# The second block's mixer: the sums of the softmaxes as a 65th column of the value products

## The chip, the cores and the metric

The kernel runs on one core of a Trainium2 chip. The metric is the device time of one execution in microseconds, as the median of three runs. TensorE (PE in the profile) multiplies and transposes, ScalarE (ACT) copies and applies functions, VectorE (DVE) does elementwise work and reductions, GpSimd (POOL) helps with powers, and the sync engine (SP) issues the loads. Each engine works through its own list in order; semaphores tie the lists together.

## The reference, cut to what matters

Two blocks of two layers each follow one another over 256 tokens of width 1024. The change lies in the mixer of the second block, which runs in both of its layers and holds three kinds of attention:

```python
# latent attention, 6 heads, causal
o_a = mla_causal_attention(q_a, k_a, kvh[..., MLA_NOPE:])
# differential attention, 6 heads: softmax(q1 k1) - lam * softmax(q2 k2), with distance slopes
p = probs(q1, k1) - lam * probs(q2, k2)
return jnp.einsum('bhqk,bhkd->bhqd', p.astype(v.dtype), v)
# block attention, 4 heads of 64; at 256 tokens it is one causal block
p = jax.nn.softmax(jnp.concatenate([s_sel, s_own], axis=-1), axis=-1).astype(v.dtype)
```

Every head has values 64 wide, and every output row is the product of the exponentials with the values, divided by the sum of the row's exponentials. A softmax row thus needs that sum, and nothing else of the sum is used. The mixer is followed by a cross attention over a memory and by an MLP. All matrix products of weights are made of three products of high and low parts; those of the attention are plain fp32.

## The kernel before, in words

**Tiling.** The 256 tokens are two tiles of 128 (t = 0, 1). Activations lie with tokens on the partitions (`X`, `H`, `proj`), and transposed where they are multiplied with weights (`HTh`, `HTl`). Weights come by DMA into a ring, ScalarE copies each piece to its high part `Wh` (L1724), VectorE subtracts to get the low part `Wl` (L2227), and TensorE makes three products a tile of rows (L922 to L924).

**The mixer.** The input projection has five blocks of columns (`IN2_BLOCKS`). ScalarE copies each out of PSUM into `proj` with the row's scale: `take_block` for blocks 0 to 3 (L1770 in the profile, since a helper records it) and `take_last` for block 4 (L2117), one instruction a tile. Between them lie the products of the latents (L983), whose results `take_heads` copies (L2130), the sums of squares of the latents on VectorE (L3021) and their scaling (L3026). The values of the differential heads lie in `proj` at column 1184, those of the block heads at column 2080, and those of the latent heads in `VV`, all 64 wide and one behind the other.

**A unit** of attention is one tile of 128 queries and up to four heads (`unit`, L362). It has kl keys: 128 for t = 0 and 256 for t = 1. The mixer has twelve units a layer: six differential ones (0 to 5), two of the block attention (6, 7), four of the latent attention (8 to 11, the last two with two heads). They hold 44 heads a layer. A unit passes through these steps, and the engines work on different units at a time:
- TensorE multiplies queries and keys (`scores`, L1075);
- VectorE adds bias or mask into `SM`, takes the maximum and writes its negative to `nb` (`mask`, L2378 to L2388);
- ScalarE takes the exponentials in `SM`, head by head, and has each summed into `sums` by the instruction's accumulator (`exps`, L1817);
- TensorE transposes the exponentials by blocks of 128 keys (`probs`, L1087), and other tiles that are due (L1097), and ScalarE copies them out of PSUM into `PT` (`copies`, L1829) or elsewhere (L1836);
- TensorE multiplies the transposed exponentials, as weights, with the values, 64 columns a head and block of keys (`values`, L1130), into one bank of PSUM;
- VectorE takes the reciprocals of `sums` and scales the product with them (`end`, L2411 to L2423).

**What sets the order.** It is written out by hand. TensorE's loop (`finish`) puts, for step i, the scores of unit i, then what `amid` names for the step, then the transposes of unit i-1, then the values of unit i-2. `amid` holds the fifth block of the input projection in quarters at steps 1 to 4 (products of 384 columns) and three products each at steps 5 to 11 whose result nobody reads (`unread`, L1653; fillers below). ScalarE's loop has the copies of unit i-1, `take_last` at steps 2 and 4, the exponentials of unit i, and weight splits after steps 0 and 4. VectorE's loop has the mask of unit i, weight splits at steps 0, 2 and 5, and the outputs of unit i-2.

Of the kernel before, what the change touches and what calls it, by code (L numbers as in the profile page):

```python
# [32 lines left out]
P = 128  # L33
# [62 lines left out]
C1W = 28 + CC * TAPS  # L96
C2 = dict(attn=0, cross=8, mem=16, mlp=24, qn=32, kvn=34)
C2W = 35
B1W = 4 * HD
B2W = HD + 4 * DIFF_D  # L100

# [9 lines left out]
def build(nc, a, out):  # L111
    ctx = ExitStack()
    with ctx:
        def sb(name, shape, dt=F32):
            return ctx.enter_context(nc.sbuf_tensor(name, shape, dt))
# [13 lines left out]
        HTh = sb("HTh", [P, KC, S], F32R)  # L129
        HTl = sb("HTl", [P, KC, S], F32R)  # L130
        proj_at = nc.sbuf_base
        proj = sb("proj", [P, T, IN2])
        scr_at = nc.sbuf_base
        scr = sb("scr", [P, 6656])

# [66 lines left out]
        CQT = QT[:, 12:15, :]  # L202
        KN = H[:, :, 0:MLA_H * NOPE].rearrange("p t (h d) -> p t h d", d=NOPE)
        QN = proj[:, :, 0:MLA_H * NOPE].rearrange("p t (h d) -> p t h d", d=NOPE)
        VV = scr[:, 22 * S:25 * S].rearrange("p (t h d) -> p t h d", t=T, h=MLA_H)
        QR = scr[:, 18 * S:21 * S].rearrange("p (t h d) -> p t h d", t=T, h=2 * MLA_H)
        KR4 = H[:, :, 768:896].rearrange("p t (n d) -> p t n d", n=4)
        MEM = scr[:, 0:T * D].rearrange("p (t d) -> p t d", t=T)
# [151 lines left out]
        def unit(t, kl, scores, bias, scale, values, dv, end, dst, kbs=None, needs=0, one=True):  # L360

            n = len(scores)  # L362
            apart = 2 if n == 2 and dv < P else 1
            return dict(t=t, kl=kl, one=one, scores=scores, bias=bias, scale=scale, values=values, dv=dv, end=end, dst=dst,
                        kbs=kbs or [P] * (kl // P), needs=needs, slots=slice(0, n * apart, apart))

        def o_bank(un, u):
# [65 lines left out]
        def diff_units(layer):  # L433
            out_ = []
            for ha, hb in ((0, 2), (1, 3), (4, 5)):
                for t in range(T):
                    kl = (t + 1) * P
                    sc, val, slopes = [], [], []
                    scale = DIFF_D ** -0.5
                    for k in range(2):  # L440
                        for h in (ha, hb):
                            r, slot = (64 * (h % 2) + k * DIFF_D, h // 2) if h < 4 else (k * DIFF_D, h - 2)
                            sc.append([(QT[r:r + DIFF_D, slot, tok(t)], QT[r:r + DIFF_D, 4 + slot, 0:kl])])
                            val.append([proj[:, kb, DV0 + h * 64:DV0 + h * 64 + 64] for kb in range(t + 1)])
                            slopes.append(-SLOPES[h] / scale)
                    dst = heads_of(H[:, t, 384:768], DIFF_H)[:, ha:hb + 1:hb - ha, :]
                    out_.append(unit(t, kl, sc, ("slopes", dist[:, t, 0:kl], slopes), scale, val, 64, ("diff", layer), dst))
            return out_

        def moba_units():  # L450
            out_ = []
            for t in range(T):
                kl = (t + 1) * P
                sc, val = [], []
                order = [2 * b + a for a in range(2) for b in range(2)]
                for h in order:
                    r = 64 * (h % 2)
                    sc.append([(QT[r:r + 64, 8 + h // 2, tok(t)], QT[r:r + 64, 10 + h // 2, 0:kl])])
                    val.append([proj[:, kb, MV0 + h * 64:MV0 + h * 64 + 64] for kb in range(t + 1)])
                scale = 64 ** -0.5  # L460
                bias = ("slopes", dist[:, t, 0:kl], [-SLOPES[DIFF_H + h] / scale for h in order])
                dst = H[:, t, 768:1024].rearrange("p (b a d) -> p a b d", a=2, b=2)
                out_.append(unit(t, kl, sc, bias, scale, val, 64, ("plain",), dst, needs=4))
            return out_
# [56 lines left out]
        for c0, slot in ((DQ0, 0), (DK0, 4)):  # L521
            t_diff.append(chunks_batch([plain_chunk(proj, c0), plain_chunk(proj, c0 + P)], slot))
            t_diff.append(chunks_batch([plain_chunk(proj, c0 + 256, 64), plain_chunk(proj, c0 + 320, 64)], slot + 2, 64))
        t_moba = [chunks_batch([plain_chunk(proj, c0 + P * b) for b in range(2)], slot)
                  for c0, slot in ((MQ0, 8), (MK0, 10))]
        qn, kn = ([plain_chunk(src, P * b) for b in range(3)] for src in (proj, H))
        qr = [plain_chunk(QR.rearrange("p t h d -> p t (h d)"), P * b) for b in range(3)]
        kr = [plain_chunk(H, 768)]
# [373 lines left out]
        def _(pe):  # L902
# [152 lines left out]
            def attention(units, extras={}, tail=None, amid={}):  # L1055
# [62 lines left out]
                def values(i):  # L1118
                    u, un = u0 + i, units[i]
                    if un["end"][0] == "nsa":  # L1120
                        return values_turned(i)
                    pe.wait_ge(pt_out, first[i] + len(un["kbs"]))
                    if un["one"] and u >= 1:
                        pe.wait_ge(o_out, u)
                    elif u >= 2:
                        pe.wait_ge(o_out, u - 1)
                    dv = un["dv"]
                    for m, vs in enumerate(un["values"]):
                        for kb, v in enumerate(vs):
                            mm = pe.matmul(PS[:, o_bank(un, u), m * dv:(m + 1) * dv],  # L1130
                                           PT[0:un["kbs"][kb], u % 2, kb, m, :], v,
                                           start=(kb == 0), stop=(kb == len(vs) - 1))
                    mm.then_inc(o_full, 1)
# [576 lines left out]
        def _(act):  # L1710
# [93 lines left out]
            def attention(units, extras={}, meanwhile={}, ahead_of={}):  # L1804
# [5 lines left out]
                def exps(i):  # L1810
                    u, un = u0 + i, units[i]
                    act.wait_ge(sm_ready, u + 1)
                    if u >= 4:
                        act.wait_ge(o_out, u - 3)
                    for m in range(len(un["scores"])):
                        row = SM[:, u % 2, m, 0:un["kl"]]
                        ins = act.activation(row, row, ACT.Exp, bias=nb[:, u % 2, m:m + 1], scale=un["scale"],  # L1817
                                             accum_out=sums[:, u % 4, m:m + 1])
                    ins.then_inc(p_ready, 1)
# [281 lines left out]
            for layer in range(LAYERS):  # L2101
                if layer == 0:
                    act.activation(st[:, 0:8], ident[:, 0:8], ACT.Exp)
                    ahead()
                    norm(col2(layer, "attn", 8), BY_HALF)

                def take_block(k):
                    c0, n = IN2_BLOCKS[k]
                    for t in range(T):
                        take(proj[:, t, c0:c0 + n], scale=row_rs[:, 0, t:t + 1])  # L2110

                def take_last(t):

                    c0, n = IN2_BLOCKS[4]
                    c.lin += 1
                    act.wait_ge(lin_full, c.lin)
                    act.activation(proj[:, t, c0:c0 + n], PS[:, 6, 0:n], ACT.Copy,  # L2117
                                   scale=row_rs[:, 0, t:t + 1]).then_inc(lin_out, 1)

                def take_heads(parts, width):  # L2120

# [16 lines left out]
                for k in range(4):  # L2138
                    c.piece += 2
                    ahead()  # L2140
                    if k == 0:
                        row_scale()
                    take_block(k)
                    if k == 1:
                        turn(t_latent(layer))
                    elif k == 2:
                        take_heads((QN, QR), NOPE + MROPE)
                        turn(t_diff)
                    elif k == 3:
                        take_heads((KN, VV), NOPE + MLA_V)  # L2150
                attention(diff_units(layer) + moba_units() + mla_units(), mix_extras,
                          {0: another, 4: another}, {2: lambda: take_last(0), 4: lambda: take_last(1)})
                turn_mix(t_mixed)
# [50 lines left out]
        def _(dve):  # L2204
# [155 lines left out]
            def attention(units, extras={}, between=None, early={}):  # L2360
# [45 lines left out]
                def end(i):  # L2406
                    u, un = u0 + i, units[i]
                    n, dv, t, dst, kind = len(un["scores"]), un["dv"], un["t"], un["dst"], un["end"]
                    dve.wait_ge(o_full, u + 1)
                    cf = coef[:, u % 2, 0:n]  # L2410
                    seq(dve.reciprocal(cf, sums[:, u % 4, 0:n]))  # L2411
                    o = heads_of(PS[:, o_bank(un, u), 0:n * dv], n)
                    tmp = otmp[:].rearrange("p (m d) -> p m d", m=4)
                    if kind[0] == "plain":
                        by = bc4(cf, dv)
                        if len(dst.shape) == 4:
                            o = o.rearrange("p (a b) d -> p a b d", a=2)
                            by = cf.rearrange("p (a b) -> p a b", a=2).unsqueeze(3).to_broadcast(list(dst.shape))
                        dve.tensor_tensor(dst, o, by, ALU.mult).then_inc(o_out, 1)
                    elif kind[0] == "diff":  # L2420
                        seq(dve.tensor_tensor(cf, cf, lam4[:, kind[1], :], ALU.mult))
                        seq(dve.tensor_tensor(tmp, o, bc4(cf, dv), ALU.mult))
                        dve.tensor_tensor(dst, tmp[:, 0:2, :], tmp[:, 2:4, :], ALU.add).then_inc(o_out, 1)  # L2423
# [575 lines left out]
            for layer in range(LAYERS):  # L2999
# [14 lines left out]
                c.piece += 2  # L3014
                ahead()
                dve.wait_ge(lin_out, base + 2)
                parts = [(t, c0, n, 2 * t + i) for t in range(T) for i, (c0, n) in enumerate(((0, QRANK), (CKV0, KVR)))]
                junk = SM[:].rearrange("p a b c -> p (a b c)")
                for t, c0, n, o in parts:
# [129 lines left out]
```

## Time and profile before

| | |
|---|---|
| time, median of 3 runs | 2428.24 us (2427.86 to 2430.18) |
| span of the profiled execution | 2425.3 us |
| TensorE busy | 2375.5 us, 98% |
| VectorE busy | 1730.3 us, 71% |
| ScalarE busy | 1447.4 us, 60% |
| mixer's attention, layer 0 / layer 1 | about 1600 to 1662 us / 2035 to 2097 us |

The time of a run is a little longer than the span of the profile, which runs from the first to the last recorded instruction. In a timeline, the first number is the start and the second the duration; where several like instructions are merged ("x4"), the duration is from the first's start to the last's end. What stands in brackets is idle time of the engine before it and what ended it. A matmul's end is modelled and lies after the start of the next one, since they are pipelined: how fast TensorE goes is read from the distance of starts. An fp32 product leaves two records, a transpose one.

### The profile page before, as it was taken

What the parts mean: (1) busy time and instruction counts of PE and PEld (TensorE: products, weight loads), DVE (VectorE), ACT (ScalarE), POOL (GpSimd) and SP (SyncE); (2) the same over time, 40 slices, a digit from 0 to 9 for tenths busy, and PEclk for the clock granted to TensorE, in tenths of its full rate; (3) what the DMA queues carried; (4) which work ended last, traced back from release to release, by engine and by line L of the source; (5) the groups of instructions that cost most, each with busy time, mean ns of one, the idle gap of its engine ahead of it and who ended that gap; (6) DMA issues with size and microseconds to landing.
All of it is one profiled execution on the core that took longest, in us unless ns stands there. A gap on an engine that the chain in (4) does not pass through costs nothing.

```text
span 2425.3 us, 32059 instructions
## 1 busy us (share of the span) xinstructions
PE 2375.5 (98%) x12122; PEld 1950.6 (80%) x12122; DVE 1730.3 (71%) x2103; ACT 1447.4 (60%) x1761; POOL 85.7 (4%) x87
## 2 busy tenths in 40 slices
PE   9899999899999999999999999999999999999998
PEld 8578888667888888888888888888878888887887
DVE  7665446758988888898888898767455565755555
ACT  6544444547777777777777777665544446554443
POOL 1100000201000000000000000001000000000000
PEclk9999999989999999999999999999999999999999
DMA  7435555327999999999999999715535542453551
GB/s 261 159 127 188 191 190 159 121 93 256 360 352 366 347 372 350 368 349 369 347 370 344 373 348 371 242 54 184 182 122 190 182 149 87 158 190 105 191 191 44
DMA packets 249705, 569.99 MB, mean 235 GB/s; under 512 B 9664, under 2 KB 20352, under 8 KB 249600
## 3 DMA queue, kind: packets, MB, share of 16 engines
q1 hardware_dynamic: 249456, 568.30, 66.6%
q8 instruction: 70, 1.15, 0.2%
q14 instruction: 35, 0.29, 0.0%
q10 hardware_dynamic: 144, 0.26, 0.0%
HBM read 562.82 MB, written 1.05 MB: 232 GB/s over the span
## 4 chain that ended last, share of the span: by engine, by line
PE 93%; DVE 4%; ACT 2%; issue 1%; POOLq 0%; POOL 0%; ACTq 0%; DVEq 0%
PE PS L922 26%; PE PS L924 26%; PE PS L923 26%; PE PS L1075 2%; PE PS L1087 1%; PE PS L1545 1%; PE PS L1130 1%; PE PS L1374 1%; PE PS L994 1%; PE PS L1194 1%; PE PS L1113 1%; ACT SM L1817 1%; PE PS L1019 1%; PE PS L1335 1%; PE PS L983 1%
## 5 line engine op out<-in xcount | busy, mean ns | idle before, releaser
L2656 DVE TENSOR_TENSOR Wl<-ring,Wh 128x2048 fp32r<-128x2048 f32 x334 | 761.8, 2298 | 101.0 <-ACT Wh L1963 101.0
L1963 ACT ACTIVATE Wh<-ring 128x2048 fp32r<-128x2048 f32 x334 | 639.9, 1919 | 127.7 <-PE PS L924 127.7
L2227 DVE TENSOR_TENSOR Wl<-ring,Wh 128x2048 fp32r<-128x2048 f32 (+2 forms) x192 | 431.3, 2251 | 283.4 <-ACT Wh L1724 282.9
L1724 ACT ACTIVATE Wh<-ring 128x2048 fp32r<-128x2048 f32 (+2 forms) x192 | 361.5, 1890 | 237.5 <-PE PS L924 236.7
L922 PE MATMUL PS<-Wh,HTh 128*128 128x512 f32 (+3 forms) x1184 | 465.6, 393 | 4.2 <-DVE Wl L2227 2.4
L924 PE MATMUL PS<-Wh,HTl 128*128 128x512 f32 (+3 forms) x1184 | 457.5, 386 | 0.0
L923 PE MATMUL PS<-Wl,HTh 128*128 128x512 f32 (+3 forms) x1184 | 456.6, 386 | 0.0
L922 PE MATMUL PS<-Wh,xgh 128*128 128x512 f32 x896 | 354.6, 396 | 1.8 <-DVE Wl L2656 1.2
L924 PE MATMUL PS<-Wh,xgl 128*128 128x512 f32 x896 | 349.8, 390 | 0.0
L923 PE MATMUL PS<-Wl,xgh 128*128 128x512 f32 x896 | 349.2, 390 | 0.0
L922 PEld LDWEIGHTS PS<-Wh,HTh 128*128 128x128 f32 x1184 | 223.6, 189 | 50.2 <-issue 4.2
L924 PEld LDWEIGHTS PS<-Wh,HTl 128*128 128x128 f32 x1184 | 223.2, 188 | 43.7
L923 PEld LDWEIGHTS PS<-Wl,HTh 128*128 128x128 f32 x1184 | 223.8, 189 | 40.8
L922 PEld LDWEIGHTS PS<-Wh,xgh 128*128 128x128 f32 x896 | 168.4, 188 | 37.4 <-DVE Wl L2656 2.0
L924 PEld LDWEIGHTS PS<-Wh,xgl 128*128 128x128 f32 x896 | 168.3, 188 | 35.8
L923 PEld LDWEIGHTS PS<-Wl,xgh 128*128 128x128 f32 x896 | 168.6, 188 | 33.4
L922 PE MATMUL PS<-Wh,hmh 128*128 128x512 f32 x448 | 176.0, 393 | 0.7 <-DVE hml L2670 0.7
L924 PE MATMUL PS<-Wh,hml 128*128 128x512 f32 x448 | 174.6, 390 | 0.0
L923 PE MATMUL PS<-Wl,hmh 128*128 128x512 f32 x448 | 174.5, 389 | 0.0
L922 PE MATMUL PS<-Wh,hTh 128*128 128x512 f32 x368 | 143.8, 391 | 0.0
L924 PE MATMUL PS<-Wh,hTl 128*128 128x512 f32 x368 | 143.4, 390 | 0.0
L923 PE MATMUL PS<-Wl,hTh 128*128 128x512 f32 x368 | 143.3, 389 | 0.0
(346 smaller groups left out, 2469.3 us busy)
## 6 DMA issues: line engine op xcount, KB each, us to landing
ring<-in_moe_w_gate SPq DMA_DIRECT2D x112, 1024.0 KB, 7.1
ring<-in_moe_w_up SPq DMA_DIRECT2D x112, 1024.0 KB, 7.6
ring<-in_moe_w_down SPq DMA_DIRECT2D x112, 1024.0 KB, 7.1
ring<-in_mlp_w SPq DMA_DIRECT2D x64, 1024.0 KB, 5.3
ring<-in_w_in SPq DMA_DIRECT2D x27, 1024.0 KB, 5.2
ring<-in_w_out SPq DMA_DIRECT2D x16, 1024.0 KB, 6.9
ring<-in_cross_wkv SPq DMA_DIRECT2D x16, 1024.0 KB, 12.3
ring<-in_ffn_w_gate SPq DMA_DIRECT2D x14, 1024.0 KB, 5.1
```

The costliest lines, as they stand in the source:

```text
L922: pe.matmul(out_, hi, high, start=start, stop=False)
L923: pe.matmul(out_, hi, low, start=False, stop=False)
L924: return pe.matmul(out_, lo, high, start=False, stop=stop)
L983: mm = pe.matmul(PS[:, bank, 0:n], lhs(kc, t), w[:, kc, c0:c0 + n], start=(kc == 0), stop=(kc == k - 1))
L994: mm = pe.transpose(PS[0:width, c.turn % 4, off:off + rows], s, ident[0:rows, 0:rows])
L1019: mm = pe.transpose(PS[:, 2 * t + half, i * P:i * P + P], src[:, t, kc * P:kc * P + P], ident[:])
L1075: mm = pe.matmul(PS[:, 2 * (u % 2) + at[m] // 2, (at[m] % 2) * S:(at[m] % 2) * S + un["kl"]], q, key, start=(k == 0), stop=(k == len(un["s ...
L1087: mm = pe.transpose(PS[0:size, 4 + x % 2, m * P:m * P + P], SM[:, u % 2, m, kb * P:kb * P + size], ident[:])
L1724: act.activation(Wh[:, i % SPLITS, 0:n], ring[:, r % RING, 0:n], ACT.Copy).then_inc(w_hi, 1)
L1963: act.activation(Wh[:, (base + i) % SPLITS, :], ring[:, (raw + i) % RING, :], ACT.Copy).then_inc(e_hi, 1)
L2227: dve.tensor_tensor(Wl[:, i % SPLITS, 0:n], ring[:, r % RING, 0:n], Wh[:, i % SPLITS, 0:n].bitcast(F32), ALU.subtract).then_inc(w_lo, 1)
L2656: dve.tensor_tensor(Wl[:, (base + i) % SPLITS, :], ring[:, (raw + i) % RING, :], Wh[:, (base + i) % SPLITS, :].bitcast(F32), ALU.subtract) ...
```

## The change

A column of ones is put behind the 64 values of each head, so that the value product gives 65 columns and the last one is the sum of the row's exponentials. What follows from that:
- `proj` is laid out anew: heads of differential and block values are 65 apart (`DVS`, `MVS`), `VV` too. `proj` grows by 12 columns a tile, which moves everything behind it in SBUF by 96 bytes.
- The copies of blocks 2, 3 and 4 of the projection become two instructions a tile, one for the heads of values and one for the rest (six more a layer).
- VectorE writes the ones with six memsets a layer, ahead of the latents' sums of squares.
- The exponentials of the mixer's units have no accumulator and no wait on `o_out`. Those of the first block and of the cross attention are as before.
- The value products have 65 columns a head, and the reciprocal reads column 64 of each head in PSUM.

```diff
@@ unit
+            wide = VW if one and end[0] != "nsa" else dv
+            return dict(t=t, kl=kl, one=one, wide=wide, summed=wide > dv, scores=scores, ...
@@ values, on TensorE
-                    dv = un["dv"]
+                    wide = un["wide"]
                     for m, vs in enumerate(un["values"]):
                         for kb, v in enumerate(vs):
-                            mm = pe.matmul(PS[:, o_bank(un, u), m * dv:(m + 1) * dv],
+                            mm = pe.matmul(PS[:, o_bank(un, u), m * wide:(m + 1) * wide],
@@ exps, on ScalarE
-                    if u >= 4:
+                    if u >= 4 and not un["summed"]:
                         act.wait_ge(o_out, u - 3)
                     for m in range(len(un["scores"])):
                         row = SM[:, u % 2, m, 0:un["kl"]]
+                        if un["summed"]:
+                            ins = act.activation(row, row, ACT.Exp, bias=nb[:, u % 2, m:m + 1], scale=un["scale"])
+                            continue
@@ ScalarE's copies of the projection
+                def spread_heads(dst, src, rs_t):
+
+                    return act.activation(dst, src.rearrange("p (h d) -> p h d", d=64), ACT.Copy, scale=rs_t)
...
+                        if k == 2:
+                            spread_heads(DVS[:, t, 0:4, 0:64], src[:, 256:512], rs_t)
+                            act.activation(proj[:, t, c0:c0 + 256], src[:, 0:256], ACT.Copy, scale=rs_t).then_inc(lin_out, 1)
+                        else:
+                            spread_heads(DVS[:, t, 4:6, 0:64], src[:, 0:128], rs_t)
+                            act.activation(proj[:, t, MQ_AT:MQ_AT + 384], src[:, 128:512], ACT.Copy,
+                                           scale=rs_t).then_inc(lin_out, 1)
...
-                    act.activation(proj[:, t, c0:c0 + n], PS[:, 6, 0:n], ACT.Copy,
-                                   scale=row_rs[:, 0, t:t + 1]).then_inc(lin_out, 1)
+                    act.activation(proj[:, t, MK_AT + 128:MK_AT + 256], PS[:, 6, 0:128], ACT.Copy, scale=rs_t)
+                    spread_heads(MVS[:, t, :, 0:64], PS[:, 6, 128:384], rs_t).then_inc(lin_out, 1)
@@ end, on VectorE
-                    seq(dve.reciprocal(cf, sums[:, u % 4, 0:n]))
-                    o = heads_of(PS[:, o_bank(un, u), 0:n * dv], n)
+                    o = heads_of(PS[:, o_bank(un, u), 0:n * un["wide"]], n)
+                    seq(dve.reciprocal(cf, o[:, :, dv] if un["summed"] else sums[:, u % 4, 0:n]))
+                    o = o[:, :, 0:dv]
@@ VectorE, ahead of the latents' sums of squares
                 dve.wait_ge(lin_out, base + 2)
+                for values_ in (DVS, MVS, VV):
+                    for t in range(T):
+                        dve.memset(values_[:, t, :, VW - 1:VW], 1.0)
```

ScalarE's list from the exponentials of unit 0 to those of unit 2, before (the row of an exponential stands for the ACTIVATE and its read of the accumulator; `Wh` is a weight split):

```order
L1817 ACTIVATE SM,sums<-SM,nb 128x128 x4
L1724 ACTIVATE Wh<-ring 128x2048
L1817 ACTIVATE SM,sums<-SM,nb 128x256 x4
L1829 ACTIVATE PT<-PS 128x512
L1836 ACTIVATE scr<-PS 128x512
L1829 ACTIVATE PT<-PS 128x512 x2
L2117 ACTIVATE proj<-PS,row_rs 128x384
L1817 ACTIVATE SM,sums<-SM,nb 128x128 x4
```

The same stretch of the changed kernel:

```order
L1827 ACTIVATE SM<-SM,nb 128x128 x4
L1733 ACTIVATE Wh<-ring 128x2048
L1827 ACTIVATE SM<-SM,nb 128x256 x4
L1841 ACTIVATE PT<-PS 128x512
L1848 ACTIVATE scr<-PS 128x512
L1841 ACTIVATE PT<-PS 128x512 x2
L2147 ACTIVATE proj<-PS,row_rs 128x128
L2121 ACTIVATE proj<-PS,row_rs 128x4x64
L1827 ACTIVATE SM<-SM,nb 128x128 x4
```

The exponentials write no sums, and the copy of the late block (L2117) has become two instructions; the order of the rest is as it was.

VectorE's list at the latents of layer 0, before (`ISA` are the sums of squares and the reads of their accumulators):

```order
L2267 TENSOR_SCALAR mean_sq<-mean_sq 128x2
L2227 TENSOR_TENSOR Wl<-ring,Wh 128x2048 x2
L3021 ISA SM,st<-proj 128x256
L3021 ISA st 128x1
L3021 ISA SM,st<-proj 128x128
```

And in the changed kernel:

```order
L2297 TENSOR_SCALAR mean_sq<-mean_sq 128x2
L2257 TENSOR_TENSOR Wl<-ring,Wh 128x2048 x2
L3050 MEMSET proj 128x6 x2
L3050 MEMSET proj 128x4 x2
L3050 MEMSET scr 128x6 x2
L3055 ISA SM,st<-proj 128x256
L3055 ISA st 128x1
L3055 ISA SM,st<-proj 128x128
```

Six memsets have been put between the two weight splits and the sums of squares.

## Rows read from the trace of the kernel before

**Rows 1.** Page, chain that ended last: share of the span by engine.
```profile
PE 93%; DVE 4%; ACT 2%; issue 1%; POOLq 0%; POOL 0%; ACTq 0%; DVEq 0%
```

**Rows 2.** Waits of TensorE in 1600 to 1662 us: total, times, longest.
```profile
PE PS L1130 <- DVE H L2419: 0.7, 1, 0.7
PE PS L1097 <- ACT PT L1829: 0.5, 2, 0.3
```

**Rows 3.** Groups of ScalarE by form: busy us, mean ns | idle before.
```profile
L1817 ACT ACTIVATION_READ_ACCUMULATOR SM<-SM,nb 128x1 f32 x200 | 38.0, 190 | 0.0
...
L1770 ACT ACTIVATE proj<-PS,row_rs 128x512 f32<-128x512 f32 x32 | 21.9, 690 | 31.9 <-PE PS L924 31.9
...
L2055 ACT ACTIVATE proj<-PS,row_rs 128x256 f32<-128x256 f32 x4 | 1.9, 470 | 3.8 <-PE PS L924 3.8
```

**Rows 4.** Timeline of ScalarE in the mixer, layer 0.
```profile
1585.23 0.33 ACT L2130 ACTIVATE proj<-PS 128x192 f32<-128x192 f32 x1 [0.28 <-PE PS L983]
...
1603.15 0.33 ACT L2130 ACTIVATE H<-PS 128x192 f32<-128x192 f32 x1 [1.66 <-PE PS L983]
...
1605.52 0.40 ACT L1817 ACTIVATE SM<-SM,nb 128x128 f32<-128x128 f32 x1
1605.82 0.20 ACT L1817 ACTIVATION_READ_ACCUMULATOR SM<-SM,nb 128x1 f32 x1
1605.91 0.40 ACT L1817 ACTIVATE SM<-SM,nb 128x128 f32<-128x128 f32 x1
...
1610.84 0.59 ACT L1829 ACTIVATE PT<-PS 128x512 f32<-128x512 f32 x1
...
1631.30 0.20 ACT L1817 ACTIVATION_READ_ACCUMULATOR SM<-SM,nb 128x1 f32 x1
```

**Rows 5.** Timeline of TensorE at units 1 and 5; last two: layer 1.
```profile
1607.14 0.34 PE L924 MATMUL PS<-Wh,HTl 128*128 128x384 f32 x1
1607.32 0.60 PE L1087 MATMUL PS<-ident,SM 128*128 128x128 f32 x4
...
1610.97 0.34 PE L924 MATMUL PS<-Wh,HTl 128*128 128x384 f32 x1
1611.57 1.06 PE L1087 MATMUL PS<-ident,SM 128*128 128x128 f32 x8 [0.26 <-ACT PT L1829]
...
1630.23 0.97 PE L1653 MATMUL PS<-HTh 128*128 128x512 f32 x3
1631.54 1.09 PE L1087 MATMUL PS<-ident,SM 128*128 128x128 f32 x8 [0.35 <-ACT SM L1817]
...
1635.87 0.96 PE L1653 MATMUL PS<-HTh 128*128 128x512 f32 x3
1636.67 0.60 PE L1087 MATMUL PS<-ident,SM 128*128 128x128 f32 x4
...
2040.64 0.34 PE L924 MATMUL PS<-Wh,HTl 128*128 128x384 f32 x1
2041.11 0.63 PE L1087 MATMUL PS<-ident,SM 128*128 128x128 f32 x4
```

**Rows 6.** Timeline of TensorE: value products of the mixer and of the cross attention.
```profile
1654.99 1.90 PE L1130 MATMUL PS<-scr,PT 128*128 128x64 f32 x16
1656.72 0.61 PE L1087 MATMUL PS<-ident,SM 128*128 128x128 f32 x4
...
1764.31 1.89 PE L1130 MATMUL PS<-proj,PT 128*128 128x256 f32 x8
```

**Rows 7.** VectorE's small groups by form; then timelines of VectorE and TensorE.
```profile
L2967 DVE TENSOR_SCALAR st<-PS 128x2 f32<-128x2 f32 x2 | 0.3, 158 | 6.1 <-PE PS L1562 6.1
...
L2840 DVE MEMSET scr<- 128x8 f32 x2 | 0.1, 65 | 0.0
...
1567.27 4.49 DVE L2227 TENSOR_TENSOR Wl<-ring,Wh 128x2048 fp32r<-128x2048 f32 x2
...
1572.49 0.82 PE L994 MATMUL PS<-ident,proj 128*128 128x128 f32 x6
1573.07 0.47 PE L922 MATMUL PS<-Wh,HTh 128*128 128x512 f32 x1
```

## What the change was predicted to do

> **What bounds the kernel now.** The page's chain of what ended last gives TensorE 93% and ScalarE 2% [rows 1]. A change that only relieves ScalarE can therefore return no more than what TensorE waits for it, so the first view is the waits of TensorE in the attention of the second block's mixer (1600 to 1662 us in layer 0; layer 1 repeats it near 2035 to 2097 us). They are few: 0.35 us for the exponentials and 0.26 us for a copy behind them (L1829) [rows 5], and then 0.5 us for two other such copies and 0.7 us for the last outputs of VectorE [rows 2]. These are idle times after modelled ends, so I take the lost time from starts, in the timeline. Between the last product of a block (L924) and the next transposes (L1087) lie 0.18 us where nothing waits (1607.14 to 1607.32) and 0.60 us at 1610.97 to 1611.57: **0.42 us lost at unit 1** [rows 5]. Between a group of three fillers (L1653) and the next transposes lie 0.80 us where nothing waits (1635.87 to 1636.67) and 1.31 us at 1630.23: **0.51 us lost at unit 5** [rows 5]. In layer 1 the same two places lose the same within 0.02 us, and there is one more, before unit 0: 2040.64 to 2041.11 is 0.47 us against 0.18, **0.29 us lost** [rows 5]. Everywhere else in the mixer TensorE starts its next instruction when the last lets it.
>
> **The accumulator.** Each exponential is two instructions, ACTIVATE and ACTIVATION_READ_ACCUMULATOR, the latter 0.190 us in the mean [rows 3]. That isn't what it costs, since the two overlap: in unit 0 (128 columns) one head's ACTIVATE starts at 1605.52 and lasts 0.40 us, the read starts at 1605.82, the next head's ACTIVATE at 1605.91 [rows 4]. The read takes 0.09 us of the pitch of 0.39 us, and without it an ACTIVATE of 0.40 us that overlaps its successor by 0.10 us (as it overlaps the read now) has a pitch of 0.30 us. Saved: 0.09 us a head, 0.37 us a unit of four heads. The mixer has 44 heads a layer, so 4.0 us of ScalarE a layer, 8 us in all. Nearly all of it goes into idle time.
>
> **What of it TensorE gets.** Unit 1: ScalarE runs the exponentials of unit 0, one weight split, the exponentials of unit 1, and then at 1610.84 the copy (L1829) that TensorE's transposes wait for [rows 4]. Two units lie ahead of that copy on ScalarE, so it comes 0.74 us earlier, more than the 0.42 us lost; what is late next is TensorE's own product. Gain 0.42 us. Unit 5: the last accumulator read is at 1631.30, and the transposes start at 1631.54 [rows 4, 5]. Ahead of it on ScalarE lie the exponentials of units 4 and 5 (0.74 us saved) and the second half of the late block's copies, which the change splits in two. The price of a split is from rows: 512 columns in one are 0.690 us, 256 columns 0.470 us [rows 3]; two of the latter with 0.10 us overlapped are 0.84 us, so 0.15 us more, and I take 0.18 us, since the halves here are unequal and the overlap varies. Left are 0.56 us against 0.51 us lost: the wait goes, with 0.05 us to spare. Unit 0 of layer 1: 0.37 us saved against 0.29 us lost. Sum: 2 x (0.42 + 0.51) + 0.29 = **2.15 us gained**.
>
> **What stays.** The copy waits [0.5 us, rows 2] are round trips: TensorE transposes, ScalarE copies, TensorE goes on; no exponential lies between. The 0.7 us on H is VectorE's scaling of a unit before the values of the next may write the one bank. Neither moves.
>
> **The 65th column.** The 66 value products a layer (one for each head and block of 128 keys), 132 in all, become 65 wide: 264 records of TensorE, as each fp32 product leaves two. Sixteen records of 64 columns take 1654.99 to 1656.72, 0.108 us each [rows 6]. Eight of 256 columns take 1.89 us with the last one's full 0.38 us: 0.216 us each, or 0.84 ns a column [rows 6]. By that slope 64 columns would be 0.054 us, half of what they take: something else than the stream sets the pitch, and the transposes, which also load 128 columns of weights each, have the same 0.11 us. So the 65th column (under 1 ns) lies beneath the weight load: 0. Exposed, it is 264 x 0.84 ns = 0.2 us. The Trainium skill ("FP8 and Floating Point Precision", TensorE Precision Notes) has true fp32 as four passes; by it and the slope of one pass at 2.4 GHz the column would be 1.7 ns a product and 0.2 us in all, the same upper end.
>
> **Other additions, at zero, with their cover.** Six memsets a layer on VectorE, ahead of the sums of squares of the latents; the nearest row, 128x8, is 65 ns [rows 7], so 0.4 us a layer at most and perhaps 0.2. Behind them stand the scaled latents, done before 1567.3, which TensorE transposes at 1572.49, and two weight splits, 1567.27 to 1571.76, with the first of them wanted at 1573.07 [rows 7]: over 3 us of cover. Without it they would cost 0.8 us in the two layers. The copies of blocks 2 and 3 are split too, 0.18 us a tile, 0.7 us a layer; but after block 2's last copy ScalarE waits 0.28 us for TensorE anyway (1585.23), and after block 3's 1.66 us (1603.15) [rows 4], so 0; uncovered, 1.4 us. The reciprocal reads four sums 65 apart out of PSUM in place of SBUF. A small operation out of PSUM is 158 ns [rows 7], no slower than its like from SBUF, so 0; it is on TensorE's path only at the last units, two a layer, and 0.06 us each would be 0.2 us. The dropped wait on o_out never ended last.
>
> **The rivals.**
> (A) The forecast, 2.15 us gained.
> (B) The gain doesn't arrive: at unit 5 only 0.05 us is to spare, and at unit 1 VectorE, which runs a weight split (half of the 4.49 us of two in [rows 7]) between the mask of unit 2 and the outputs of unit 0, becomes what is late. Then unit 5's 0.51 us stays in both layers, or all does: 0 to 1.1 us gained, 2427.1 to 2428.2.
> (C) Slower: the 65-column records leave the pace of the weight load. Heads 1 and 3 of a unit now start at columns 65 and 195 of the bank, and values at odd words. If such a record ran at half speed, 65 columns would take 0.110 us, still the pace of now and only 0.3 to 0.5 us in all. It decides from 26 ns a record (264 x 0.026 = 6.9 us, less 2.15). If stream and load stopped overlapping, 0.108 + 0.055, it is 14.5 us less 2.15: 2440.6. For it speaks only that no row has an odd start; against it, the factor of two in hand. The Trainium skill ("Advanced Engine Details and Errata", PSUM Cachelines) says PSUM lines hold two fp32 values and that patterns which aren't contiguous slow matmuls; each output here is contiguous in itself, only its start is odd. By that rule at its worst, half speed, the result is the 0.3 to 0.5 us above.
> (D) Faster by over 0.2%: all that TensorE loses in the two mixers to ScalarE and VectorE would have to go. That is 2.15 us and the waits that stay, 1.2 us a layer by [rows 2]: 4.6 us as idle time, and a little more by starts. It barely reaches 0.2%, and I see no mechanism.
> (E) The change doesn't do what it says: the order of instructions has the exponentials without sums, so I give it nothing.
>
> **How the numbers follow.** The profiled execution spans 2425.3 us, and the median of three runs is 2428.24, so 2.9 us lie around the span. 2425.3 - 2.15 = 2423.15 in the profile, and 2426.1 as a time. (A) 0.66; (B) 0.20; (C) 0.09 with its small form counted in (A) and (B); (D) 0.05. The three runs lie between 2427.86 and 2430.18, so a median may move by a microsecond. The range reaches from 1.5 us more gain than forecast, less that scatter, to (B) with the exposed columns, memsets and splits (up to 1.8 us slower than now): 2423.6 to 2430.0. 0.2%, about what a measurement of this kernel can tell from no change, is 4.9 us: faster 0.05, same 0.86, slower 0.09.
>
> **What would show it.** The profile of the changed kernel should have 88 fewer accumulator reads, exponentials of one unit 0.30 us apart where they have 128 columns, about 0.18 us between L924 and the transposes of unit 1, and about 0.80 us between the fillers and those of unit 5; the waits on L1829's copies and on H should be as before; sixteen 65-column records should take 1.73 us. If those take over 2 us, it is (C). If the exponentials end earlier and the transposes of units 1 and 5 don't start earlier, it is (B), and the releaser names what took the place. The argument would be wrong if stages outside the mixer changed, since only addresses behind the projection's tile move there (by 96 bytes).

## The result, and the profile after

The changed kernel takes **2458.19 us** (median of 4 runs, 2453.68 to 2462.35), the kernel before 2428.05 us beside it (2426.87 to 2430.18). The ratio is 1.0125, interval 1.0108 to 1.0143: slower by 30 us, where 2 us of gain were forecast and the range ended at 2430.0.

The page of the changed kernel, its span, its busy times, and the chain that ended last:

```profile
span 2460.6 us, 31971 instructions
...
PE 2412.9 (98%) x12122; PEld 1953.4 (79%) x12122; DVE 1734.7 (70%) x2115; ACT 1441.8 (59%) x1685; POOL 85.2 (3%) x87
...
PE 94%; DVE 4%; ACT 1%; issue 1%; DMA 0%; SPq 0%; POOLq 0%; POOL 0%; ACTq 0%; DVEq 0%
```

TensorE is busy 37 us longer than before (2375.5), and its share of the chain went up by 1% and ScalarE's down by 1% [rows 1]. Nothing new is waited for; TensorE itself takes longer.

**The mixer did what was forecast.** Timeline of TensorE in the mixer of layer 0 (start, duration, group), then its waits in 1631 to 1695 us:

```profile
1643.71 0.34 PE L933 MATMUL PS<-Wh,HTl 128*128 128x384 f32 x1
1643.89 1.04 PE L1096 MATMUL PS<-ident,SM 128*128 128x128 f32 x8
...
1662.41 0.96 PE L1662 MATMUL PS<-HTh 128*128 128x512 f32 x3
1663.25 1.10 PE L1096 MATMUL PS<-ident,SM 128*128 128x128 f32 x8
...
1686.71 1.90 PE L1139 MATMUL PS<-scr,PT 128*128 128x65 f32 x16
1688.44 0.61 PE L1096 MATMUL PS<-ident,SM 128*128 128x128 f32 x4
```

```profile
PE PS L1139 <- DVE H L2450: 0.7, 1, 0.7
PE PS L1106 <- ACT PT L1841: 0.5, 2, 0.3
```

At unit 1, 0.18 us lie between the last product and the transposes (0.60 before), and at unit 5 0.84 us between the fillers and the transposes (1.31 before) [rows 5]. Sixteen value records of 65 columns take 1.73 us, as sixteen of 64 did [rows 6]. The two waits that were to stay have stayed [rows 2]. In layer 1 it is the same: 0.17 us at unit 0 (0.47 before) and 0.20 us at unit 1, and at unit 5 again 0.84. Of ScalarE, a group by form, then the timeline:

```profile
L1829 ACT ACTIVATION_READ_ACCUMULATOR SM<-SM,nb 128x1 f32 x112 | 20.9, 187 | 0.0
```

```profile
1631.48 0.36 ACT L2121 ACTIVATE proj<-PS,row_rs 128x128 f32<-128x128 f32 x1
1631.73 0.58 ACT L2138 ACTIVATE proj<-PS,row_rs 128x384 f32<-128x384 f32 x1
...
1638.29 1.28 ACT L1827 ACTIVATE SM<-SM,nb 128x128 f32<-128x128 f32 x4
```

There are 112 accumulator reads in place of 200 [rows 3]. Four exponentials of 128 columns take 1.28 us; with 0.40 us for the last one [rows 4], they start (1.28 - 0.40) / 3 = 0.29 us apart. A copy of 512 columns in two pieces ends 0.83 us after its start (0.25 to the second start, and its 0.58) against 0.69 in one piece.

**Where the time went.** I cut the execution at two products that can be found in each trace: the first of the mixture of experts (`xgh`), and the first of the second block (416 columns). Before:

```profile
561.21 0.50 PE L922 MATMUL PS<-Wh,xgh 128*128 128x512 f32 x1 [0.60 <-DVE xgl L2234]
...
1551.55 0.43 PE L922 MATMUL PS<-Wh,HTh 128*128 128x416 f32 x1
```

After:

```profile
568.00 0.50 PE L931 MATMUL PS<-Wh,xgh 128*128 128x512 f32 x1 [0.61 <-DVE xgl L2264]
...
1584.32 0.43 PE L931 MATMUL PS<-Wh,HTh 128*128 128x416 f32 x1
```

| stretch | before | after | difference |
|---|---|---|---|
| first block, up to the experts | 561.2 | 568.0 | +6.8 |
| the experts | 990.3 | 1016.3 | **+26.0** |
| second block, to the end of the span | 873.7 | 876.3 | +2.5 |

No line of the experts was touched by the change. Timeline of TensorE there, before (first and last of 18 records that follow one another):

```profile
900.13 0.39 PE L922 MATMUL PS<-Wh,hmh 128*128 128x512 f32 x1
...
903.98 0.39 PE L924 MATMUL PS<-Wh,hml 128*128 128x512 f32 x1
```

After (first and last of 19):

```profile
899.65 0.40 PE L931 MATMUL PS<-Wh,hmh 128*128 128x512 f32 x1
...
903.87 0.40 PE L931 MATMUL PS<-Wh,xgh 128*128 128x512 f32 x1
```

The records start 3.85 / 17 = 0.2265 us apart before and 4.22 / 18 = 0.2344 us apart after, with no wait between them. The groups of wide products by form (busy us, mean ns), before:

```profile
L922 PE MATMUL PS<-Wh,HTh 128*128 128x512 f32 x1088 | 433.1, 398 | 3.3 <-DVE Wl L2227 1.7 <-ACT proj L1770 1.0 <-DVE scr L2976 0.5
L922 PE MATMUL PS<-Wh,xgh 128*128 128x512 f32 x896 | 354.6, 396 | 1.8 <-DVE Wl L2656 1.2 <-DVE xgl L2234 0.6
L923 PE MATMUL PS<-Wl,xgh 128*128 128x512 f32 x896 | 349.2, 390 | 0.0
L922 PE MATMUL PS<-Wh,hTh 128*128 128x512 f32 x368 | 143.8, 391 | 0.0
```

After, with the weight load of one of them:

```profile
L931 PE MATMUL PS<-Wh,HTh 128*128 128x512 f32 x1088 | 433.1, 398 | 3.3 <-DVE Wl L2257 1.7 <-ACT proj L1779 1.0 <-DVE scr L3007 0.5
L931 PE MATMUL PS<-Wh,xgh 128*128 128x512 f32 x896 | 359.4, 401 | 1.3 <-DVE Wl L2687 0.6 <-DVE xgl L2264 0.6
L932 PE MATMUL PS<-Wl,xgh 128*128 128x512 f32 x896 | 355.2, 396 | 0.0
L931 PE MATMUL PS<-Wh,hTh 128*128 128x512 f32 x368 | 146.3, 398 | 0.0
```

```profile
L932 PEld LDWEIGHTS PS<-Wl,xgh 128*128 128x128 f32 x896 | 168.9, 189 | 38.4
```

The products whose stationary operand is `HTh` are the same to the nanosecond. Those with `xgh`, `hmh` and `hTh` (and with their low parts) are slower, by 5 to 7 ns each, while their weight load takes the 188 to 189 ns that it took before. What sets the two kinds apart is where the operand lies: `HTh` has a tile of its own ahead of `proj`, and the others are views of `scr`, behind `proj`. `proj` grew by 96 bytes, so of the stationary operands of these wide products they, and only they, lie 96 bytes further from the weights `Wh` and `Wl`. The names can mislead here: the kernel's weights `Wh` and `Wl` are the moving operand, which streams through TensorE, and the activations are the stationary one, which is loaded ahead of each product.

**The sum closes.** The experts have 896 x 3 + 448 x 3 = 4032 such records, and 26.0 us over 4032 is 6.4 ns each. Counted the other way: about 3740 of them are followed directly by another such product, and in the mean of all these pairs the starts are 0.2272 us apart before and 0.2342 after, 7.0 ns more, which makes 26.2 us. The first block has 336 with `hTh` (2.2 us at that price), the second 768 (4.9 us). With 2.5 us of gain in the mixers that makes 2.2 + 26.0 + 4.9 - 2.5 = 30.6 us, against 30.1 between the medians. The two profiled spans differ by 35.3 us, and the other 4.6 lie in the first block, where the granted clock of TensorE isn't the same from one execution to the next. It is 1.00 in every stretch from 600 us on; in 50 to 150 and 450 to 550 us, where TensorE has many small products and is idle 3 to 8 us of 50, it falls for a part of the time from 2.4 to 1.2 GHz. TensorE by stretch (start:end, length, busy, count, clock, DMA share, GB/s), before and after:

```profile
50.00:100.00 50.00, 42.84 (x412) 0.93 0.40 125
100.00:150.00 50.00, 47.25 (x390) 0.90 0.33 114
```

```profile
50.00:100.00 50.00, 43.51 (x366) 0.83 0.38 119
100.00:150.00 50.00, 47.25 (x417) 0.86 0.30 98
```

The other two stretches, before and in a kernel of the experiments below whose first block differs only in where one tile lies (`hTl`):

```profile
450.00:500.00 50.00, 42.46 (x440) 0.86 0.55 174
500.00:550.00 50.00, 47.38 (x286) 0.86 0.20 64
```

```profile
450.00:500.00 50.00, 41.98 (x451) 0.93 0.55 174
500.00:550.00 50.00, 45.63 (x302) 0.97 0.19 64
```

How long it stays low differs between executions of one kernel too: of the changed kernel's four runs, two had a mean clock of 0.992 (2453.68 and 2454.22 us) and two 0.988 (2462.16 and 2462.35). So below I compare stretches. Where nothing moved that they use, they agree between the kernels to 0.2 us in the experts (990.2 to 990.4) and to 0.4 us in the second block (873.4 to 873.8); one trace was kept of each kernel.

### The profile page after: what moved, and what is told of

It reads as the page before. It is cut to its first block, busy times and chain, and to the rows that moved or that the text cites. A ratio compares the mean times of both kernels' runs of the same rounds, so it can differ in the third digit from the quotient of the medians.

```text
span 2460.6 us, 31971 instructions
## 1 busy us (share of the span) xinstructions
PE 2412.9 (98%) x12122; PEld 1953.4 (79%) x12122; DVE 1734.7 (70%) x2115; ACT 1441.8 (59%) x1685; POOL 85.2 (3%) x87
## 4 chain that ended last, share of the span: by engine, by line
PE 94%; DVE 4%; ACT 1%; issue 1%; DMA 0%; SPq 0%; POOLq 0%; POOL 0%; ACTq 0%; DVEq 0%
PE PS L931 27%; PE PS L933 26%; PE PS L932 26%; PE PS L1084 2%; PE PS L1139 1%; PE PS L1554 1%; PE PS L1096 1%; PE PS L1383 1%; PE PS L1003 1%; PE PS L1203 1%; PE PS L1122 1%; PE PS L1028 1%; PE PS L1344 1%; PE PS L992 1%; PE PS L1327 1%
## 5 line engine op out<-in xcount | busy, mean ns | idle before, releaser
L932 PE MATMUL PS<-Wl,xgh 128*128 128x512 f32 x896 | 355.2, 396 | 0.0
L933 PE MATMUL PS<-Wh,xgl 128*128 128x512 f32 x896 | 355.1, 396 | 0.0
```

What stands on the lines that cost most here:

```text
L932: pe.matmul(out_, hi, low, start=False, stop=False)
L933: return pe.matmul(out_, lo, high, start=False, stop=stop)
```

## The experiments

**The layout without the change.** The kernel before, with 12 unused columns in `proj`:

```diff
-        proj = sb("proj", [P, T, IN2])
+        proj = sb("proj", [P, T, IN2 + 12])
```

> The kernel before with 12 unused columns added to each tile of proj, as in the changed kernel, and nothing else: everything behind proj moves by 96 bytes, so that scr starts 32 bytes past a multiple of 64. Theory P (place): products whose stationary operand lies in scr (xgh, xgl, hmh, hml, hTh, hTl; 5136 records) go from a pitch of 0.227 to 0.234 us, 5136 x 7.3 ns = 37 us slower, near 2465 us; products with HTh keep theirs. Rival M (mixer): the loss comes from the wider values, the memsets or the split copies: no change, 2428 us. Rival C (code): the longer instruction lists of the changed kernel are at fault: no change here either.

Measured: 2459.87 us, ratio 1.0128 (1.0111 to 1.0145). The experts take 1016.31 us, as in the changed kernel, and the second block 878.64, 4.9 more than before: the loss without the mixer's gain. **96 bytes of unused memory cost what the change cost.**

**A rounder size.** The changed kernel, with the width of `proj` rounded so that `scr` moves by 128 bytes instead of 96:

```diff
-W2 = -(-(MV_AT + MOBA_H * VW) // 4) * 4
+W2 = -(-(MV_AT + MOBA_H * VW) // 16) * 16
```

> The changed kernel with proj rounded up to a multiple of 16 columns (2352 for 2348), so that everything behind it moves by 128 bytes instead of 96 and scr starts at a multiple of 64 again; same instructions, same order. Theory P: the loss is gone and what was forecast for the change remains, 2.15 us less than before, near 2426 us. Rivals M and C: still near 2458 us.

Measured: 2451.97 us, ratio 1.0100 (1.0083 to 1.0117); the experts 1011.26 us, so 5.2 ns a record in place of 6.4. `scr` starts at a multiple of 64 bytes again, and I had expected the loss to go: it didn't, so being a multiple of 64 is no cure.

**Two operands alone.** The kernel before, with `hTh` and `hTl`, the stationary operand of the dense MLPs, 32 bytes further on in `scr`, and nothing else moved:

```diff
-        hTh = over_scr("hTh", 1024, [P, 2, 4, S])
-        hTl = over_scr("hTl", 3072, [P, 2, 4, S])
+        hTh = over_scr("hTh", 1032, [P, 2, 4, S])
+        hTl = over_scr("hTl", 3080, [P, 2, 4, S])
```

> The kernel before with hTh and hTl alone moved by 32 bytes inside scr (the stationary operands of the down products of the dense MLPs, 1104 records); nothing else moves and no tile grows. Theory P: 1104 x 7.3 ns = 8 us slower, near 2436 us, pitch of these records 0.234 us, and all others as before. If the shift matters through anything else behind proj (SM, PT, constants), no change.

Measured: 2437.37 us, ratio 1.0041 (1.0026 to 1.0055), the experts 990.35 us as before, the second block 878.28 (+4.5 for 768 records, 5.9 ns each). Timeline of TensorE (first and last of 36 records):

```profile
1899.64 0.40 PE L922 MATMUL PS<-Wh,hTh 128*128 128x512 f32 x1
...
1907.81 0.40 PE L924 MATMUL PS<-Wh,hTl 128*128 128x512 f32 x1
```

They start 0.2334 us apart, where `HTh` still has 0.227. So the delay goes with where the operand itself lies. It is no effect of the changed mixer, nor of the stage. The price of the records, with 336 of them in the first block, makes 6.5 of the 9.5 us between the medians; the rest is in the first block, which took 5.8 us longer than before in the profiled executions where 2.0 are due to records, and where the clock differs too (0.86 and 0.83 in 50 to 150 us).

**A pad behind `scr`.**

```diff
         scr = sb("scr", [P, 6656])
+        pad = sb("pad", [P, 8])
```

> The kernel before with 32 unused bytes between scr and SM: scr stays, everything behind it (SM, PT, ident, constants, small tiles) moves by 32 bytes. The stationary operands moved are SM (fp32 transposes), PT (value products) and rows_h/rows_l's low half, none of them in the wide products. Theory P: at most 1 us slower, 2428 to 2429 us. If any tile off a multiple of 64 costs, several us slower.

Measured: 2428.51 us, ratio 0.9997 (0.9985 to 1.0009). So 32 bytes on the tiles behind `scr` cost nothing that can be seen.

**Everything moved, or all but the weights.** First 128 bytes ahead of the ring of weights, so that stationary and moving operands move together; then 32 bytes ahead of `Wh` and 224 behind `Wl`, so that the weights move by 32 and the rest by 256:

```diff
+        pad = sb("pad", [P, 32])
         ring = sb("ring", [P, RING, PIECE])
```

> The kernel before with 128 unused bytes ahead of the first big tile (ring): everything, moving and stationary operands, moves by 128 bytes together. Theory R (relative): what counts is the distance of the stationary from the moving operand's start within 256 bytes, which stays 0: no change, 2428 us. Theory A (absolute): the stationary operand must start 128 past a multiple of 256: now all wide products are off, those with HTh too: 8688 records x 4.9 ns (the 0.2317 less 0.2268 us of the shift by 128) = 43 us slower, near 2470 us.

```diff
+        pad = sb("pad", [P, 8])
         Wh = sb("Wh", [P, SPLITS, PIECE], F32R)
...
         Wl = sb("Wl", [P, SPLITS, PIECE], F32R)
+        pad2 = sb("pad2", [P, 56])
```

> The kernel before with Wh and Wl (the moving operands) moved by 32 bytes and everything behind them by 256, which leaves it where it was within 256. Theory R: every wide product has its operands 32 bytes off each other, 8688 records x 6.6 ns = 57 us slower, near 2485 us, with HTh's pitch at 0.233 us too. Theory A: the stationary operands haven't moved within 256: no change, 2428 us.

Measured: the first 2427.44 us, ratio 0.9993 (0.9983 to 1.0002), the experts 990.33. The second 2474.47 us, ratio 1.0184 (1.0168 to 1.0199), the slowest of all, since now `HTh` is hit too. Group by form:

```profile
L924 PE MATMUL PS<-Wh,HTh 128*128 128x512 f32 x1088 | 438.7, 403 | 3.1 <-DVE Wl L2229 1.8 <-ACT proj L1772 0.7 <-DVE scr L2978 0.5
```

Moving both costs nothing, and moving the moving operand costs about as much a record as moving the stationary one: **it is the distance between the two that counts, not an address.** All 8400 records of 512 columns are hit, and 44.7 us (2428 x 0.0184) over 8400 are 5.3 ns each. The mixer's products of 384 columns, with the same operands displaced by the same 32 bytes, aren't: in some 80 pairs that follow one another directly the starts are 0.1750 us apart before and 0.1746 here.

**The change with the distance kept.** The changed kernel, with 32 columns added to `proj` instead of 12, so that `scr` moves by 256 bytes; and the same with the exponentials' accumulator and their wait on `o_out` put back, which nobody needs then:

```diff
-W2 = -(-(MV_AT + MOBA_H * VW) // 4) * 4
+W2 = IN2 + 32
```

> The changed kernel with proj at 2368 columns (for 2348), so that everything behind it moves by 256 bytes instead of 96; same instructions. A shift by 128 bytes left most of the loss, with the pitch of the products out of scr at 0.232 us. Theory Q (256): what counts is where the stationary operand starts within 256 bytes; in the kernel before all of Wh, Wl, HTh and scr start 128 past a multiple of 256. Then a shift by 256 brings the pitch back to 0.227 us, and what is left is the forecast gain, 2.15 us: near 2426 us. Rival S (size): the loss grows or falls with where scr lies in a larger pattern: 2440 to 2460 us.

```diff
-                    if u >= 4 and not un["summed"]:
+                    if u >= 4:
...
-                            ins = act.activation(row, row, ACT.Exp, bias=nb[:, u % 2, m:m + 1], scale=un["scale"])
+                            ins = act.activation(row, row, ACT.Exp, bias=nb[:, u % 2, m:m + 1], scale=un["scale"],
+                                                 accum_out=sums[:, u % 4, m:m + 1])
```

> The same with the accumulator of the exponentials kept (its sums are written and not read), so that only the layout, the wider values, the memsets, the split copies and the reciprocal out of PSUM of the change remain. By the forecast all of these cost nothing and the accumulator is worth 2.15 us: as the kernel before, 2428 us, and less the waits of units 1 and 5 as before. If the extra copies on ScalarE cost, up to 1 us slower than before.

Measured: **2424.74 us** (11 runs), ratio 0.9985 (0.9976 to 0.9994), the one version that beats the kernel before, by 1.5 to 5.8 us; and with the accumulator 2429.02 us (11 runs), ratio 0.9994 (0.9985 to 1.0003). The experts take 990.32 and 990.39 us, the loss is gone. The second block takes 871.23 us without the accumulator and 873.82 with it, 873.75 before. So the 65th column, the memsets, the split copies and the sums read from PSUM together cost nothing that can be seen, and the whole gain of 2.5 us comes from leaving out the accumulator and the wait that went with it. The two weren't put back one by one.

**Other distances, and one operand of the pair.** `hTh` and `hTl` moved by 64, 128 and 192 bytes as they were by 32 above, and then `hTl` alone by 32:

```diff
-        hTl = over_scr("hTl", 3072, [P, 2, 4, S])
+        hTl = over_scr("hTl", 3080, [P, 2, 4, S])
```

> The kernel before with hTh and hTl alone moved by 64 bytes inside scr. If every start that isn't the moving operand's within 256 bytes costs (theory R), the pitch of these 1104 records is between 0.231 and 0.234 us; if only starts off a multiple of 64 cost fully, it is nearer to 0.227. Time 2428 + 1104 x (pitch - 0.2268).

> hTh and hTl alone moved by 128 bytes. Theory R: 0.2317 us as for all of scr in the shift by 128, so about 5 us more. If the 0.2317 us came from the other tiles behind proj, 0.2268 us.

> hTh and hTl alone moved by 192 bytes, the mirror of 64. If the cost falls with the distance to the next multiple of 256, as for 64 bytes; if it grows with the offset, more.

> The kernel before with hTl alone moved by 32 bytes, hTh in place. One in three loads of these products then starts 32 bytes off. If the clash is between a load and the product that streams while it is loaded, the interval before the hTl product (from Wl x hTh to Wh x hTl) is about 0.24 us or more and the other two stay at 0.227; if the clash is within a product's own operands, the interval after it is the long one. Time about 2.5 to 3 us more, below what one look can tell.

Measured: 2432.62, 2434.43, 2433.64 and 2427.58 us, one run each beside 2429.07 of the kernel before. These times say little, for their clocks are 0.992, 0.990, 0.987 and 0.993: the last is the kernel of the second pair of clock rows above. It reached the experts 4 us earlier than the kernel before (557.2 us), and by its time alone it looks free. The second block, with its clock of 1.00 throughout, tells them apart. All distances together, with the cost of a record from the stretch (its excess over 873.75, or over 990.34 in the experts, by 768 or 4032 records):

| moved against the weights by | from | cost of a record |
|---|---|---|
| 32 bytes | second block 878.28 | 5.9 ns |
| 32, `hTl` alone | second block 878.38 | 6.0 ns |
| 64 | second block 878.76 | 6.5 ns |
| 96 | experts 1016.3; second block of the pad alone 878.64 | 6.4; 6.4 ns |
| 128 | second block 877.94; experts 1011.26 | 5.5; 5.2 ns |
| 192 | second block 875.19 | 1.9 ns |
| 224 (the weights by 32) | experts 1012.78 | 5.6 ns |
| 0, 256, or both by 128 | experts 990.3 to 990.4 | 0 |

Timeline of TensorE with 192 bytes (first and last of 36):

```profile
1899.81 0.39 PE L922 MATMUL PS<-Wh,hTh 128*128 128x512 f32 x1
...
1907.82 0.39 PE L924 MATMUL PS<-Wh,hTl 128*128 128x512 f32 x1
```

8.01 / 35 = 0.2289 us apart. A difference of 0.3 us in the second block is 0.4 ns a record, so its figures for 32, 64 and 128 bytes (5.5 to 6.5 ns) are hardly told apart, while 192 bytes stand clearly below them, and 64 bytes to the other side (192 is 64 short of 256) don't cost what 64 bytes cost. And with `hTl` alone displaced (twelve triples), with the groups by form:

```profile
1891.22 0.40 PE L922 MATMUL PS<-Wh,hTh 128*128 128x512 f32 x1
...
1899.62 0.40 PE L922 MATMUL PS<-Wh,hTh 128*128 128x512 f32 x1
```

```profile
L923 PE MATMUL PS<-Wl,hTh 128*128 128x512 f32 x368 | 147.1, 400 | 0.0
L922 PE MATMUL PS<-Wh,hTh 128*128 128x512 f32 x368 | 145.6, 396 | 0.0
L924 PE MATMUL PS<-Wh,hTl 128*128 128x512 f32 x368 | 143.2, 389 | 0.0
```

8.40 / 36 = 0.2333 us a record: one displaced operand of three makes a triple as slow as three do. That rules out that each product pays for its own operand alone, since then it would be a third. The longest record is L923, and it is under its stream that the operand of L924, `hTl`, is loaded:

```profile
1851.07 0.40 PE L923 MATMUL PS<-Wl,hTh 128*128 128x512 f32 x1
1851.07 0.19 PEld L924 LDWEIGHTS PS<-Wh,hTl 128*128 128x128 f32 x1
1851.31 0.39 PE L924 MATMUL PS<-Wh,hTl 128*128 128x512 f32 x1
```

One start is told to 10 ns in these rows and the effect is 6, but the second block has about 250 of each interval, and their means tell them apart (before: 0.2267, 0.2267 and 0.2269 us):

| from the start of | to the start of | operand loaded meanwhile | mean, us | above before |
|---|---|---|---|---|
| L922 | L923 | `hTh` | 0.2322 | 5.5 ns |
| L923 | L924 | `hTl`, the displaced one | 0.2388 | 12.1 ns |
| L924 | L922 | `hTh` | 0.2285 | 1.5 ns |

Most of the loss lies where I had expected it for a clash between the stream of one product and the load for the next: in the interval in which `hTl` is loaded, and not in the one in which it is used. That fits a clash in reading SBUF, but it doesn't show one, and it isn't all: the interval before it, in which nothing displaced is streamed or loaded by these rows, pays 5.5 ns.

## Why the prediction was wrong

- **The bound** was read rightly: TensorE is the chain, and only what it waits for can be won. It follows also that whatever slows TensorE's own pace is paid in full, and that side I didn't work out.
- **The accumulator**: 0.09 us a head was right (starts 0.29 us apart, forecast 0.30), 88 reads fewer.
- **The gain of TensorE**, 2.15 us, was nearly right: 0.42 us at unit 1 and 0.47 of 0.51 at unit 5 in the changed kernel, and 2.5 us for the second block where the layout is repaired. That version's profile spans 2423.0 us, and 2423.15 was forecast; so close a hit is luck, since one execution differs from the next by more (2421.68 to 2428.67 us in its 11 runs). Rival (B), that the gain doesn't arrive, is refuted.
- **The 65th column** is free: 1.73 us for sixteen records, as said. Rival (C), where all my chance of slower by this column lay, is refuted: the sign came true and its mechanism didn't.
- **Memsets, split copies, sums out of PSUM**: nothing, as said, by the kernel with the accumulator put back. The split itself was 0.14 us dearer, forecast 0.15 to 0.18. The range's upper end took 1.8 us for these when exposed, with the columns; its own prices (0.2, 0.8 and 1.4 us) add up to 2.4, a slip that changes nothing here.
- **The step that failed** is the last sentence: "The argument would be wrong if stages outside the mixer changed, since only addresses behind the projection's tile move there (by 96 bytes)". The move was seen and named and then given no term in the sum, no rival and no chance, as though an address had no price. Its price is 6.4 ns a record, 5136 records, 33 us: fifteen times the gain. No row of the trace before shows a product of 512 columns with a displaced operand, so it couldn't have been sized there. But the bound could have been worked out: TensorE's wide records are 8400, each nanosecond on them is 8.4 us, and a term with such a lever deserved a rival of its own and a range that isn't 6 us wide.

## What to carry to other kernels

A change of layout moves every tile behind it. Before a size is changed, list what moves against what, count the instructions that read the moved tiles, and pad the tile so that the distances stay (here to 256 bytes: 160 bytes a partition more than the change's own 96 bought back 33 us). After it, compare first the stages that the change didn't touch, cut at instructions that both traces have, and compare starts, since a pace that changed by 3% shows in no wait.

## What the runs showed of the hardware

- Back-to-back fp32r products of 512 columns, each with a load of 128 columns of weights, start about 0.227 us apart (0.2272 in the mean of the experts) where the stationary and the moving operand begin at the same place modulo 256 bytes, and 0.229 to 0.234 us apart at other distances. The cost isn't monotonic: 5.9, 6.5, 6.4, 5.2 to 5.5, 1.9 and 5.6 ns at 32, 64, 96, 128, 192 and 224 bytes. Products of 384 columns showed no cost at 224 bytes (0.1750 and 0.1746 us). Other types and other distances weren't tried.
- The Trainium skill ("TensorE: Matmul & The Clock Gate", Step-by-step: what each phase is for) has two independent read ports of SBUF, one for the stream and one for the weight load, and says that loading the next tile's weights takes no read bandwidth from the running product. The runs agree that stream and load overlap (both start at 1851.07). They add that the pace of the overlapped pair still depends on where the two operands lie against each other, by up to 3%; whether that is read bandwidth, no run here shows.
- One displaced operand in three costs as much as three (6.0 and 5.9 ns a record), with most of it in the interval in which that operand is loaded (12.1 ns). Which part of the chip this comes from stays open.
- A product of 65 fp32 columns that starts at an odd column of its bank costs the same 0.108 us a record as one of 64.
